# A decoder layer in float32 pairs: the first norm's weight row loaded once and spread by two TensorE products

## The chip, the cores and the metric

One core of a Trainium2 chip runs the kernel. The time is device microseconds of one execution; for each kernel the median of several runs is given.

## The reference

Input x has 512 tokens of 1024 channels. One layer is computed, all in float32:

```
h = rms_norm(x, norm_mix_pre)                     # x * rsqrt(mean(x*x) + 1e-6) * weights
z = h @ w_in                                      # 1024 x 10240, ten parts of 1024 columns
y_a, y_c, y_s = three causal branches of z        # short conv, long conv, spatial gating
m = (sum over branches of sigmoid(gate) * (y @ w_branch)) @ w_out
x = x + rms_norm(m, norm_mix_post)
h = rms_norm(x, norm_ffn_pre)
x = x + rms_norm(square(relu(h @ w_ff1)) @ w_ff2, norm_ffn_post)
```

The change touches only the first line. The first of the ten parts of `w_in` that the kernel multiplies is `s_v` (the `v` of the spatial gating).

## The kernel before

Every large product is made from two rounded parts of each operand, hi and lo, in three TensorE products (hi*hi, hi*lo, lo*hi; lines 1440 to 1444). Weights come in **units** of 128x1024 (512 KB) through two `raw` slots. ScalarE rounds a unit to `w_hi` (`split_hi`, line 607, its copy in line 605), VectorE subtracts and writes `w_lo` (`split_lo`, line 962, line 958), and a ring of four such pairs feeds TensorE. A unit's `raw` slot may be loaded again once its `w_lo` is written.

The start of the program, up to the first matmul of `s_v`, goes for each token tile c of 128 tokens through all engines:

- SyncE (line 420 on) loads x tile 0 into `resid` (its memory is called conf in the profile), then the weight row of the first norm, broadcast from one row of 4 KB in memory to 128 partitions, `row[0]` (its memory is glu; 512 KB are moved, line 429), then units 0 and 1, x tile 1, and with waits for `w_lo` the next units and tiles.
- ScalarE sums the squares of the tile (`sum_squares`, line 629), rounds a unit, and rounds the turned tile to `a_hi` (`turned_hi`, line 633). The order is written out in lines 642 to 654: for tile 0 squares, unit 0, `a_hi`, unit 1.
- POOL (GpSimd) makes rstd from the sum in two small steps (lines 512 and 516).
- VectorE multiplies x by rstd and by the weight row (lines 989 to 991, into `by_token`, whose memory is wide), makes `w_lo`, and `a_lo` of the turned tile (line 980).
- TensorE first runs 20 products of constants (`keep_warm`, line 1512), then turns tile 0 (8 transposes of 128x128, `turn`, line 1477), runs 6 more products of constants, and then blocks of `s_v`: a block (c, n) is token tile c by unit n, 6 matmuls. The order of the blocks and where the turns of tiles 1, 2, 3 stand between them is a table (`V_BLOCKS`, `V_TURNS`, line 49): (0, 0), (0, 1), turn of tile 1, (0, 2), and so on. The blocks of unit n wait for its `w_lo`, those of tile c for its `a_lo`.

Each engine goes through its own list in order. After `s_v` follow the other parts of `w_in`, the branches, `w_out`, and the MLP, which uses a Strassen-like scheme of seven products instead of eight on quarter blocks.

Of the kernel before, what the change touches and what calls it, by code (L numbers as in the profile page):

```python
# [25 lines left out]
F32 = mybir.dt.float32  # L26
F32R = mybir.dt.float32r
ALU = mybir.AluOpType
ACT = mybir.ActivationFunctionType

P = 128
D = 1024
# [3 lines left out]
HALF = D // 2  # L36
# [8 lines left out]
RAW = 2  # L45


WARM, WARM_AGAIN = 20, 6
V_BLOCKS = ((0, 0), (0, 1), (0, 2), (1, 0), (1, 1), (1, 2), (0, 3), (1, 3), (2, 0), (2, 1), (2, 2), (2, 3),
            (3, 0), (3, 1), (3, 2), (3, 3))  # L50
V_TURNS = {(0, 1): 1, (1, 2): 2, (2, 1): 3}
# [11 lines left out]
ROW_MIX_PRE, ROW_MIX_POST, ROW_FFN_PRE, ROW_FFN_POST = range(4)  # L63
# [151 lines left out]
def build(nc, x_d, units_d, cols_d, rows_d, ws_d, bs_d, out_d):  # L215
    kept_d = nc.dram_tensor("mixed_kept", (SEQ, D), F32, kind="Internal").ap()
    with ExitStack() as ctx:
# [10 lines left out]
        def sem(name):  # L228
            return ctx.enter_context(nc.semaphore(name))
# [9 lines left out]
        a_hi = sb("a_hi", [P, KT, SEQ], F32R)  # L239
# [6 lines left out]
        by_token = wide[:, :].rearrange("p (c n) -> p c n", c=CH)  # L246
# [5 lines left out]
        row = [glu_flat[:, n * D:(n + 1) * D] for n in range(3)]  # L252
# [5 lines left out]
        resid = conf_flat[:, :].rearrange("p (c n) -> p c n", c=CH)  # L258
# [16 lines left out]
        ones = sb("ones", [P, P], F32R)  # L275
# [6 lines left out]
        rstd = sb("rstd", [P, 4 * CH])  # L282
        power = sb("power", [P, CH])
        ps = ctx.enter_context(nc.psum_tensor("ps", [P, 8, 512], F32))
# [41 lines left out]
        x_loaded = [sem(f"x_loaded{n}") for n in range(CH)]  # L326
        x_again = sem("x_again")
        rows_loaded = sem("rows_loaded")
        rows_again = sem("rows_again")
        cols_loaded = sem("cols_loaded")  # L330
        spatial_loaded = [sem(f"spatial_loaded{n}") for n in range(2)]
# [8 lines left out]
        normed = sem("normed")  # L340
# [80 lines left out]
        def _(sp):  # L421
# [3 lines left out]
            def x_load(c):  # L425
                sp.dma_start(resid[:, c, :], x_d[c * P:(c + 1) * P, :]).then_inc(x_loaded[c], 16)

            x_load(0)
            sp.dma_start(row[0], rows_d[ROW_MIX_PRE:ROW_MIX_PRE + 1, :].to_broadcast([P, D])
                         ).then_inc(rows_loaded, 16)  # L430
            for slot in range(RAW):
                load(slot, slot)
            x_load(1)
# [169 lines left out]
        def _(act):  # L603
# [3 lines left out]
            def split_hi(u, into=None, free=True):  # L607

                act.wait_ge(raw_loaded[u.raw], u.loads())
                if free and u.first >= RING:  # L610
                    act.wait_ge(unit_done, u.times(1, 1 - RING))
                copy_hi(w_hi[:, u.ring, :] if into is None else into,
                        raw[:, u.raw, :]).then_inc(w_hi_ready, 1)
# [19 lines left out]
            def turned_hi(n, c, dst, banks):  # L633

                for g in range(2):
                    act.wait_ge(turned, 2 * n + g + 1)
                    copy_hi(dst[:, 4 * g:4 * g + 4, c * P:(c + 1) * P],
                            ps[:, banks + g, :].rearrange("p (k t) -> p k t", k=4)
                            ).then_inc(act_hi_ready, 1)


            for c in range(CH):
                act.wait_ge(x_loaded[c], 16)
                sum_squares(c, resid[:, c, :].rearrange("p (b n) -> p b n", b=2),
                            ps[:, 2 * c:2 * c + 2, :])
                if c == 0:
                    split_hi(Count(0))
                elif c < CH - 1:
                    split_hi(Count(c + 1))
                    turned_hi(c, c, a_hi, 2 * c)  # L650
                if c == 0:
                    turned_hi(0, 0, a_hi, 0)
                    split_hi(Count(1))
            turned_hi(CH - 1, CH - 1, a_hi, 2 * (CH - 1))


# [298 lines left out]
        def _(dve):  # L955
# [26 lines left out]
                       hi[:, 4 * g:4 * g + 4, c * P:(c + 1) * P]).then_inc(act_lo_ready, 1)  # L982


            dve.wait_ge(rows_loaded, 16)
            for c in range(CH):
                dve.wait_ge(x_loaded[c], 16)
                dve.wait_ge(rstd_ready, c + 1)
                nc.vector.scalar_tensor_tensor(out=by_token[:, c, :], in0=resid[:, c, :],
                                               scalar=rstd[:, c:c + 1], in1=row[0], op0=ALU.mult,  # L990
                                               op1=ALU.mult).then_inc(normed, 1)
                if c < CH - 1:
                    split_lo(Count(c + 1 if c else 0))
                turned_lo(c, c, a_hi, a_lo, 2 * c)
                if c == 0:
                    split_lo(Count(1))
# [165 lines left out]
            for j in range(KT):  # L1162
# [19 lines left out]
                for t in SILU_TILES.get(j, ()):  # L1182
                    dve.wait_ge(silu_th, t + 1)
                    nc.vector.scalar_tensor_tensor(out=nrm[:, t, :], in0=conf[:, t, :], scalar=1.0,
                                                   in1=nrm[:, t, :], op0=ALU.add,
                                                   op1=ALU.mult).then_inc(silu, 1)
# [44 lines left out]
            for c in range(CH):  # L1231
                if c == CH - 1:
                    x_turned(c - 1)
                for half in range(2):
# [7 lines left out]
                                               scalar=rstd[:, CH + 2 * c:CH + 2 * c + 1],  # L1242
                                               in1=resid[:, c, :], op0=ALU.mult,
# [193 lines left out]
        def _(pe):  # L1437
# [74 lines left out]
            def keep_warm(many):  # L1512
                for _ in range(many):
                    nc.tensor.matmul(ps[:, 7, :], ones[:, :], ones[:, :].unsqueeze(1).to_broadcast([P, CH, P]),
                                     start=True, stop=True)

            pe.wait_ge(consts_ready, 4)
            keep_warm(WARM)
            pe.wait_ge(consts_ready, 5)
            turn(0, 0, 0)  # L1520
            keep_warm(WARM_AGAIN)
            for c, n in V_BLOCKS:
                pe.wait_ge(act_lo_ready, 2 * c + n // 2 + 1)
                ready(Count(U_V + n))
# [199 lines left out]
```

## Time and profile before

| | before |
|---|---|
| median of 3 runs | 977.22 us (977.0 to 978.5) |
| the profiled execution, its time | 977.74 us |
| its span, first to last instruction | 976.0 us |
| TensorE (PE) busy | 959.6 us, 98% |
| VectorE (DVE) busy | 717.2 us, 73% |
| ScalarE (ACT) busy | 422.6 us, 43% |
| GpSimd (POOL) busy | 121.0 us, 12% |
| memory traffic | 135.43 MB read, 4.19 MB written |
| mean granted clock of TensorE | 0.996 |

The profile shows one execution. Busy time is counted per instruction; PEld is TensorE's loading of the stationary operand, and SPq, POOLq and the like are the engines' queues, which issue DMAs. A chain of waits is followed back from an instruction to what released it.

### The profile page before, as it was taken

The numbers are of one execution on the slowest core, as the hardware profiler recorded it, in microseconds if no ns is written. First come the engines' busy times: TensorE is split into PE (matmuls) and PEld (weight loads), VectorE is DVE, ScalarE is ACT, GpSimd is POOL, SyncE is SP. The second block draws the span as 40 slices with busy tenths as digits, with TensorE's granted clock in tenths as the row PEclk, the third lists the DMA queues.
The fourth block names the chain that finished last, engine by engine and source line by source line (L and its number), as shares of the span: only waits on it lengthen the run. The fifth ranks groups of instructions, "written<-read, shape, count | busy, mean of one in ns | idle before, by whom it ended". The sixth has DMA issues, their size and how long they took to land.

```text
span 976.0 us, 13542 instructions
## 1 busy us (share of the span) xinstructions
PE 959.6 (98%) x4910; PEld 819.0 (84%) x4910; DVE 717.2 (73%) x839; ACT 422.6 (43%) x526; POOL 121.0 (12%) x146
## 2 busy tenths in 40 slices
PE   8999999999999999999999999998899999999996
PEld 6888888888888888888888888898779989989985
DVE  5458889889888888886585434587775785796698
ACT  5333332333233222224374223466736745754673
POOL 1100000001000001122200000131122112111112
PEclk9999999999999999999999999999999999999999
DMA  6324222232232222224225333479989979989665
GB/s 244 96 87 130 92 91 92 89 110 91 95 104 86 87 86 86 86 87 139 99 86 216 108 107 108 172 169 283 235 197 222 229 197 233 195 195 259 140 177 141
DMA packets 39196, 140.23 MB, mean 144 GB/s; under 512 B 4464, under 2 KB 4592, under 8 KB 39152
## 3 DMA queue, kind: packets, MB, share of 16 engines
q1 hardware_dynamic: 28608, 101.88, 30.6%
q0 software_dynamic: 9728, 34.61, 19.3%
q10 hardware_dynamic: 816, 3.15, 0.9%
q8 instruction: 28, 0.46, 0.2%
q14 instruction: 16, 0.13, 0.0%
HBM read 135.43 MB, written 4.19 MB: 143 GB/s over the span
## 4 chain that ended last, share of the span: by engine, by line
PE 86%; DMA 5%; DVE 4%; ACT 3%; issue 1%; POOL 0%; DVEq 0%; POOLq 0%; SPq 0%; ACTq 0%
PE ps L1440 24%; PE ps L1442 24%; PE ps L1444 24%; PE ps L1607 4%; PE ps L1611 4%; PE ps L1609 4%; DMA raw_d<-units_in 4%; DVE w_lo L958 2%; ACT w_hi L605 1%; DVE h_lo L958 1%; DMA raw<-units_in 1%; PE ps L1483 1%; DVE wide L1306 0%; ACT h_hi L605 0%; PE ps L1548 0%
## 5 line engine op out<-in xcount | busy, mean ns | idle before, releaser
L1440 PE MATMUL ps<-a_hi,w_hi 128*128 128x512 f32 x576 | 225.4, 391 | 0.0
L1442 PE MATMUL ps<-a_lo,w_hi 128*128 128x512 f32 x576 | 224.2, 389 | 0.0
L1444 PE MATMUL ps<-a_hi,w_lo 128*128 128x512 f32 x576 | 224.1, 389 | 0.0
L958 DVE TENSOR_TENSOR w_lo<-raw,w_hi 128x1024 fp32r<-128x1024 f32 x124 | 153.1, 1237 | 89.5 <-ACT w_hi L605 89.1
L605 ACT ACTIVATE w_hi<-raw 128x1024 fp32r<-128x1024 f32 x124 | 130.2, 1056 | 188.5 <-PE ps L1444 111.0
L1034 DVE SCALAR_TENSOR_TENSOR conf<-glu,cols,conf (+1 forms) x240 | 186.9, 779 | 27.5 <-DVE conf L1034 26.4
L1442 PEld LDWEIGHTS ps<-a_lo,w_hi 128*128 128x128 f32 x576 | 108.2, 188 | 22.7 <-issue 0.5
L1440 PEld LDWEIGHTS ps<-a_hi,w_hi 128*128 128x128 f32 x576 | 108.1, 188 | 22.7 <-DVE w_lo L958 0.2
L1444 PEld LDWEIGHTS ps<-a_hi,w_lo 128*128 128x128 f32 x576 | 108.1, 188 | 22.5
L958 DVE TENSOR_TENSOR w_lo<-glu,w_hi 128x1024 fp32r<-128x1024 f32 x56 | 67.9, 1224 | 41.6 <-ACT w_hi L605 41.6
L1440 PE MATMUL ps<-w_hi,h_hi 128*128 128x512 f32 x224 | 87.8, 392 | 1.6 <-DVE wide L1306 0.8
L1442 PE MATMUL ps<-w_lo,h_hi 128*128 128x512 f32 x224 | 87.2, 390 | 0.0
L1444 PE MATMUL ps<-w_hi,h_lo 128*128 128x512 f32 x224 | 87.2, 389 | 0.0
L605 ACT ACTIVATE w_hi<-glu 128x1024 fp32r<-128x1024 f32 x56 | 58.6, 1054 | 46.8 <-PE ps L1444 20.4
L1607 PE MATMUL ps<-x_plain_hi,w_hi 128*128 128x256 f32 x256 | 73.7, 288 | 4.0 <-DVE h L1281 2.5
L1611 PE MATMUL ps<-x_plain_hi,w_lo 128*128 128x256 f32 x256 | 73.1, 286 | 0.0
L1609 PE MATMUL ps<-x_plain_lo,w_hi 128*128 128x256 f32 x256 | 73.1, 285 | 0.0
L576 POOL DMA_DIRECT2D glu<-units_in x40 | 34.8, 878 | 183.4 <-DVE w_lo L958 138.6
L1607 PE MATMUL ps<-x_diff_hi,w_hi 128*128 128x256 f32 x192 | 54.7, 285 | 1.2 <-DVE x_diff_lo L958 0.8
L1609 PE MATMUL ps<-x_diff_lo,w_hi 128*128 128x256 f32 x192 | 54.3, 283 | 0.0
L1611 PE MATMUL ps<-x_diff_hi,w_lo 128*128 128x256 f32 x192 | 54.3, 283 | 0.0
L1607 PEld LDWEIGHTS ps<-x_plain_hi,w_hi 128*128 128x128 f32 x256 | 49.8, 195 | 5.1 <-DVE h L1281 2.9
(175 smaller groups left out, 1655.7 us busy)
## 6 DMA issues: line engine op xcount, KB each, us to landing
raw<-units_in SPq DMA_DIRECT2D x128, 512.0 KB, 3.3
glu<-units_in POOLq DMA_DIRECT2D x40, 512.0 KB, 6.7
glu<-units_in SPq DMA_DIRECT2D x24, 512.0 KB, 5.3
raw_d<-units_in POOLq DMA_DIRECT2D x24, 512.0 KB, 8.3
raw_v<-units_in SPq DMA_DIRECT2D x16, 512.0 KB, 5.6
raw_d<-units_in SPq DMA_DIRECT2D x8, 512.0 KB, 3.9
conf<-x_in SPq DMA_DIRECT2D x4, 512.0 KB, 4.7
conf<-x_in ACTq DMA_DIRECT2D x1, 2048.0 KB, 7.9
```

Source lines behind the costliest of these rows:

```text
L576: pool.dma_start(slots[slot], units_d[source(u, added=True)], accum_op=ALU.add).then_inc(raw_added[slot], 16)
L605: return nc.scalar.activation(dst, src, ACT.Copy, scale=scale)
L958: return nc.vector.tensor_tensor(dst, src, hi, ALU.subtract)
L1034: nc.vector.scalar_tensor_tensor(out=conf[:, tile, :], in0=glu[:, tile, k:k + SEQ], scalar=cols[:, tile, COL_CONF + k:COL_CONF + k + 1], i ...
L1440: nc.tensor.matmul(ps[:, bank, :], left_hi, right_hi, start=first, stop=False, skip_group_check=on_top)
L1442: nc.tensor.matmul(ps[:, bank, :], left_hi, right_lo, start=False, stop=False, skip_group_check=on_top)
L1444: return nc.tensor.matmul(ps[:, bank, :], left_lo, right_hi, start=False, stop=final, skip_group_check=on_top)
L1483: mm = nc.tensor.transpose(ps[:, banks + g, k * P:(k + 1) * P], by_token[:, c, at:at + P], ident[:, :])
L1607: nc.tensor.matmul(out, w_hi[:, u % RING, w], hi[:, k, :], start=not free and k == 0, stop=False, skip_group_check=free)
L1609: nc.tensor.matmul(out, w_hi[:, u % RING, w], low[:, k, :], start=False, stop=False, skip_group_check=free)
L1611: mm = nc.tensor.matmul(out, w_lo[:, u % RING, w], hi[:, k, :], start=False, stop=k == CH - 1, skip_group_check=free)
```

## The change

It does four things. The weight row is loaded as one row of 4 KB to partition 0 of `row[1]`, ahead of all other loads. TensorE spreads it: after 4 products of constants it waits for that load and multiplies a column of ones (one partition) by the row in two products of 512 columns, into PSUM banks 4 and 5; then 8 products of constants, the turn of tile 0, 4 products of constants (instead of 20, the turn, and 6). VectorE's norm product of tile 0 reads the weights from these banks; for tiles 1 to 3 it reads `row[0]` as before, which ScalarE copies from the banks behind the squares of tile 1. And ScalarE rounds unit 1 ahead of `a_hi` of tile 0 instead of behind it.

```diff
-WARM, WARM_AGAIN = 20, 6
+WARM = 4, 8, 4
...
+        row_spread = sem("row_spread")
+        row_ready = sem("row_ready")
...
+            sp.dma_start(row[1][0:1, :], rows_d[ROW_MIX_PRE:ROW_MIX_PRE + 1, :]).then_inc(rows_loaded, 16)
             x_load(0)
-            sp.dma_start(row[0], rows_d[ROW_MIX_PRE:ROW_MIX_PRE + 1, :].to_broadcast([P, D])
-                         ).then_inc(rows_loaded, 16)
...
                 if c == 0:
                     split_hi(Count(0))
+                    split_hi(Count(1))
+                    turned_hi(0, 0, a_hi, 0)
                 elif c < CH - 1:
+                    if c == 1:
+                        nc.scalar.activation(row[0].rearrange("p (b n) -> p b n", b=2), ps[:, 4:6, :],
+                                             ACT.Copy).then_inc(row_ready, 1)
                     split_hi(Count(c + 1))
                     turned_hi(c, c, a_hi, 2 * c)
-                if c == 0:
-                    turned_hi(0, 0, a_hi, 0)
-                    split_hi(Count(1))
...
-            dve.wait_ge(rows_loaded, 16)
+            two = "p (b n) -> p b n"
             for c in range(CH):
                 dve.wait_ge(x_loaded[c], 16)
                 dve.wait_ge(rstd_ready, c + 1)
-                nc.vector.scalar_tensor_tensor(out=by_token[:, c, :], in0=resid[:, c, :],
-                                               scalar=rstd[:, c:c + 1], in1=row[0], op0=ALU.mult,
-                                               op1=ALU.mult).then_inc(normed, 1)
+                if c == 0:
+                    dve.wait_ge(row_spread, 1)
+                else:
+                    dve.wait_ge(row_ready, 1)
+                nc.vector.scalar_tensor_tensor(out=by_token[:, c, :].rearrange(two, b=2),
+                                               in0=resid[:, c, :].rearrange(two, b=2),
+                                               scalar=rstd[:, c:c + 1],
+                                               in1=row[0].rearrange(two, b=2) if c else ps[:, 4:6, :],
+                                               op0=ALU.mult, op1=ALU.mult).then_inc(normed, 1)
...
             pe.wait_ge(consts_ready, 4)
-            keep_warm(WARM)
+            keep_warm(WARM[0])
+            pe.wait_ge(rows_loaded, 16)
+            for b in range(2):
+                mm = nc.tensor.matmul(ps[:, 4 + b, :], ones[0:1, :].bitcast(F32), row[1][0:1, b * HALF:(b + 1) * HALF],
+                                      start=True, stop=True)
+            mm.then_inc(row_spread, 1)
+            keep_warm(WARM[1])
             pe.wait_ge(consts_ready, 5)
             turn(0, 0, 0)
-            keep_warm(WARM_AGAIN)
+            keep_warm(WARM[2])
```

ScalarE's list from its second row on, before (names are the memories of the program; `glu` holds the weight row):

```order
2 L630 ACTIVATE ps,sumsq<-conf 128x1024
3 L605 ACTIVATE w_hi<-raw 128x1024
4 L605 ACTIVATE a_hi<-ps 128x4x128 x2
5 L605 ACTIVATE w_hi<-raw 128x1024
6 L630 ACTIVATE ps,sumsq<-conf 128x1024
7 L605 ACTIVATE w_hi<-raw 128x1024
8 L605 ACTIVATE a_hi<-ps 128x4x128 x2
```

The same place now (the lines have moved by one or more):

```order
2 L631 ACTIVATE ps,sumsq<-conf 128x1024
3 L606 ACTIVATE w_hi<-raw 128x1024 x2
4 L606 ACTIVATE a_hi<-ps 128x4x128 x2
5 L631 ACTIVATE ps,sumsq<-conf 128x1024
6 L653 ACTIVATE glu<-ps 128x1024
7 L606 ACTIVATE w_hi<-raw 128x1024
8 L606 ACTIVATE a_hi<-ps 128x4x128 x2
```

The rounding of unit 1 now stands ahead of the two of `a_hi`, and the copy of the row stands between the squares of tile 1 and the rounding of unit 2.

TensorE's list at its start, before:

```order
1 L1514 MATMUL ps<-ones 128x512 x20
2 L1483 MATMUL ps<-ident,wide 128x128 x8
3 L1514 MATMUL ps<-ones 128x512 x6
4 L1440 MATMUL ps<-w_hi,a_hi 128x512
5 L1442 MATMUL ps<-w_lo,a_hi 128x512
```

And now:

```order
1 L1523 MATMUL ps<-ones 128x512 x4
2 L1530 MATMUL ps<-glu,ones 128x512 x2
3 L1523 MATMUL ps<-ones 128x512 x8
4 L1492 MATMUL ps<-ident,wide 128x128 x8
5 L1523 MATMUL ps<-ones 128x512 x4
6 L1449 MATMUL ps<-w_hi,a_hi 128x512
7 L1451 MATMUL ps<-w_lo,a_hi 128x512
```

The two products that spread the row, and eight products of constants, stand between the first four and the turn of tile 0. VectorE's list has the same instructions in the same order; only the sources and the waits of the norm products differ.

## Rows read from the trace of the kernel before

**Rows 1.** Busy time by engine in one stretch, then clock, DMA share, GB/s.

```profile
16.00:649.00 633.00, 633.00 (x2888) 526.28 (x2889) 464.53 (x584) 225.92 (x310) 58.83 (x63) 1.00 0.33 107
```

**Rows 2.** The chain of waits, 0 to 60 us: start, duration, what.

```profile
1.72 6.17 DMA raw<-units_in
7.91 1.06 ACT w_hi L605
...
9.94 0.95 ACT w_hi L605
...
13.39 1.30 DVE wide L989
14.73 1.09 PE ps L1483 x8
15.96 0.47 PE ps L1440
```

**Rows 3.** The timeline, 0 to 22 us: start, duration, engine, line, what.

```profile
0.81 0.38 SPq L426 DMA_DIRECT2D conf<-x_in  x1
...
1.25 0.42 SPq L429 DMA_DIRECT2D glu<-rows_in  x1
...
1.38 6.72 PE L1514 MATMUL ps<-ones 128*128 128x512 f32 x20 [1.38 <-POOL ones L498]
...
4.32 1.03 ACT L630 ACTIVATE ps<-conf 128x1024 f32<-128x1024 f32 x1 [2.23 <-DMA conf<-x_in]
...
6.58 1.28 DVE L989 SCALAR_TENSOR_TENSOR wide<-conf,rstd,glu 128x1024 f32<-128x1024 f32 x1 [6.58 <-POOL rstd L516]
...
8.87 1.07 ACT L605 ACTIVATE a_hi<-ps 128x512 fp32r<-128x512 f32 x2
8.99 1.22 DVE L958 TENSOR_TENSOR w_lo<-raw,w_hi 128x1024 fp32r<-128x1024 f32 x1 [1.13 <-ACT w_hi L605]
...
10.14 1.28 DVE L958 TENSOR_TENSOR a_lo<-ps,a_hi 128x512 fp32r<-128x512 f32 x2
...
10.88 0.50 PE L1440 MATMUL ps<-w_hi,a_hi 128*128 128x512 f32 x1 [0.41 <-DVE a_lo L958]
...
11.34 1.22 DVE L958 TENSOR_TENSOR w_lo<-raw,w_hi 128x1024 fp32r<-128x1024 f32 x1
...
13.48 1.06 ACT L605 ACTIVATE w_hi<-raw 128x1024 fp32r<-128x1024 f32 x1 [1.57 <-DMA raw<-units_in]
...
13.93 0.39 PE L1444 MATMUL ps<-w_hi,a_lo 128*128 128x512 f32 x1
...
15.42 1.09 ACT L605 ACTIVATE a_hi<-ps 128x512 fp32r<-128x512 f32 x2 [0.88 <-PE ps L1483]
...
16.05 1.29 DVE L958 TENSOR_TENSOR a_lo<-ps,a_hi 128x512 fp32r<-128x512 f32 x2 [0.24 <-ACT a_hi L605]
```

**Rows 4.** Landings: units 0 and 1; the row broadcast; the spatial weights.

```profile
DMA to landing us min/median/max: 6.2/6.6/7.0
...
DMA to landing us min/median/max: 5.2/5.2/5.2
...
DMA to landing us min/median/max: 2.0/2.1/2.6
```

**Rows 5.** The stretch between the landings of the broadcast and of unit 0.

```profile
6.50:7.90 1.40, 1.40 (x7) 0.95 (x6) 1.28 (x1) 0.00 (x0) 0.00 (x0) 1.00 1.03 421
```

**Rows 6.** The first products of constants, by tile; a float32 product, from the chain.

```profile
L1514 PE MATMUL ps<-ones x8: 628/628/792, 1.4 to 4.5; 128*128 128x512 f32 x8
...
441.50 0.86 PE ps L1568 x2
```

**Rows 7.** Groups on VectorE by form: one subtraction from SBUF, one from PSUM.

```profile
L958 DVE TENSOR_TENSOR v_lo<-wide,v_hi 128x512 fp32r<-128x512 f32 x8 | 5.5, 686 | 0.0
...
L958 DVE TENSOR_TENSOR a_lo<-ps,a_hi 128x512 fp32r<-128x512 f32 x8 | 5.1, 685 | 4.5 <-ACT a_hi L605 4.5
```

**Rows 8.** Busy time and clock in a later stretch.

```profile
687.00:691.00 4.00, 3.36 (x17) 3.37 (x18) 2.06 (x3) 2.56 (x3) 1.50 (x3) 0.63 0.46 137
```

## The prediction

> **What bounds the kernel.** I read the busy time by stretches first. From 16 to 649 us the matrix engine (PE) is busy the whole of 633 us [rows 1]. A microsecond won before 16 us is therefore kept that long, and behind that the waits are counted from work that starts earlier by as much. So only the first 16 us are in question, in which the change lies. There the chain of waits [rows 2] is to be read: it leads from the landing of the first weight unit (issued 1.72, landed 7.89) over ScalarE (w_hi of unit 0, a_hi of token tile 0, w_hi of unit 1 in 0.95 us, then the squares of tile 1) and the two small POOL steps to VectorE's norm product of tile 1 (13.39), the turn of tile 1 on PE (14.73) and block (0, 2) at 15.96, from which PE is never idle. Last I read the timeline of the same stretch [rows 3], for what stands beside that chain and how much room it has. I name the tiles 0 to 3 and units 0, 1, 2 by their numbers.
>
> **Part by part: the loads.** The 512 KB broadcast leaves SyncE's queue, and a 4 KB load goes in front. x tile 0 was issued at 0.81 and the next DMA at 1.25, so tile 0 is issued 0.44 us later and, its 3.5 us being unchanged, lands at 4.75 instead of 4.3 [rows 3]. Units 0 and 1 are issued as before but 508 KB less stand ahead of them. The broadcast landed at 1.25 + 5.2 = 6.45, 2.15 us behind tile 0; unit 0 came at 7.89, 1.45 later, and unit 1, issued about 0.44 behind it, at about 2.17 + 7.0 = 9.2, 1.3 later [rows 4]. With the broadcast gone I add the last two steps to 4.75: unit 0 at 6.2, unit 1 at 7.5. If the second transfer in the stream is slow wherever it comes from, its step is 2.15, and unit 1 lands at 8.2; if nothing is won, 9.2 or, with the extra issue, 9.6. I take 7.5, since the stream ran at 421 GB/s behind the broadcast [rows 5].
> The Trainium skill (DMA: Bandwidth & Descriptors, Specifications) puts the ceiling of the fabric at 435 GB/s; an estimate from it is 1.2 us for the removed 512 KB, and unit 1 would land at 9.2 + 0.44 - 1.2 = 8.4. By that rule the sum below would be -0.4 us instead of -0.75; the rows show a slower broadcast than that (2.15 us).
>
> **The spread.** Four warm-up products end at 1.38 + 4 x 0.44 = 3.1; at this point matmuls stand 0.44 us apart (8 of them from 1.4 to 4.5), which is the 1.2 GHz level, and the remaining 12 of the 20 take what is left of 6.72 us, so some 0.23 to 0.27 us [rows 3, 6]. The granted clock column shows 1.00 from the start; the level I take from the spacing. The 4 KB row lands 2.0 us (the shortest landing that I found) to 3.5 us (tile 0's own) after 0.81 [rows 3, 4], so between 2.8 and 4.3; I take 3.2. No row has a product over one partition: the nearest is a float32 product of 128x512, 0.86 us at full clock [rows 6], so two take 1.72, or 3.44 at half clock. With the clock up at 4.5 the spread ends at about 5.7, with it down all the time at 6.6. VectorE needs it at 7.02 (below): no cost, with 0.4 to 1.3 us to spare. Behind it 8 warm-ups (1.8 us) end at about 7.5, ahead of the turn at 8.36: none either.
>
> **The norm product of tile 0.** It waited for rstd at 6.58, 2.26 us after ScalarE began on tile 0; it starts 0.44 later, at 7.02. It reads PSUM now: the same subtraction of 128x512 takes 686 ns from SBUF and 685 ns from PSUM [rows 7], so I price that at nothing, with the range 0 to 0.07.
> The Trainium skill (VectorE: DVE Perf Modes, The TRN2 errata) gives a PSUM source 62 cycles more than an SBUF one, which at its clock is an estimate of 0.065 us; the sum by it would be -0.68 in place of -0.75. The pair of rows does not agree with it, and the measurement decides.
> Norm to turn is 1.34 us and turn to a_hi 0.69 (13.39, 14.73, 15.42) [rows 2, 3]: the turn of tile 0 starts at 8.36 and a_hi at 9.05, against 8.87 before: **+0.18, rounded 0.2 us**.
>
> **The split moved on ScalarE.** w_hi of unit 1 stood between a_hi and the squares of tile 1 and took 0.95 us of the chain [rows 2]. Now it lies ahead of a_hi. Squares of tile 0 run 4.75 to 5.9, w_hi of unit 0 6.2 to 7.2, of unit 1 7.5 to 8.5; a_hi is not ready before 9.05, so this costs nothing with 0.55 us of room. **-0.95 us.** The squares of tile 1 thus start 0.75 earlier, at about 10.0. Tile 1 itself has to be in: it landed before 10.8 and comes earlier too.
>
> **The copy of the row.** 1.06 us of ScalarE (a 128x1024 copy, the 7.91 row), behind the squares, from 11.2 to 12.3. The norm product of tile 1 waits for it, but also for rstd, at 13.39 - 0.75 = 12.64. Hidden, by 0.3 us. Behind the copy waits w_hi of unit 2, which was held by its load: 4.49 us after w_lo of unit 0 began (8.99, 13.48). That subtraction now starts right behind the norm product, at 8.25, so w_hi of unit 2 starts at 12.74 and ends at 13.8; VectorE comes to it at 13.84. Hidden, by a hair.
>
> **PE's two blocks before the turn of tile 1.** a_lo of tile 0 starts 0.63 behind a_hi (15.42, 16.05), at 9.68, 0.46 earlier than before; block (0, 0) starts 0.74 behind, at 10.42, and block (0, 1), which follows w_lo of unit 1, also moves by 0.46. Its last matmul began at 13.93 and now begins at 13.47, ahead of the turn of tile 1 at 13.98. VectorE ended w_lo of unit 1 at 12.56, now 12.1, before 12.64. So the 0.75 stays whole: block (0, 2) starts at 15.21 instead of 15.96.
>
> **Sum**: +0.2 - 0.95 = **-0.75 us**. The profiled execution took 977.74 us over a span of 976.0, so 976.99 of its kind; it stands 0.52 above the median of the runs, 977.22, and the forecast is set against that: **976.5 us**. That is 0.08%. A measurement of this kernel can tell about 0.2%, 1.95 us, so no change should be seen.
>
> **Rivals.**
> (a) *Unit 1 lands late and ScalarE stands on it.* The split of unit 1 now blocks a_hi. From a landing after 8.1 on, each microsecond costs one; at 8.83 the gain is gone, and at 9.2 a_hi starts at 10.2: +0.4 us, 977.6. For it: the stream is full from 2 us on, and tile 0 goes out later. Against it: half a megabyte fewer are in front. Chance 0.15; half of it at the 8.2 to 8.4 above, about 976.8.
> (b) *Slower: PE's own queue.* The two products and 8 warm-ups stand ahead of the turn of tile 0, on an engine that at first runs at 1.2 GHz, and PE may idle while the row loads. From 3.2 us there is work of 3.43 us at full and 6.86 at half clock. If the level rises at T, it ends at 3.2 + 3.43 + (T - 3.2)/2: ahead of 8.36 up to T = 6.7, and the whole gain is lost at T = 8.2. If it stays low until 10 us or more, the turn starts at 10.1 (1.7 late), and blocks (0, 0) and (0, 1), 12 matmuls, take 0.2 us more each: another 2.4, so 4.2 us over the forecast, 980.7. For it: before, PE had run without a stop from 1.38 when the spacing changed at 4.5, and now it has a wait at 3.1. Against it: the wait is 0.1 us if the row lands at 3.2. Chance 0.09.
> (c) *Tile 0 is not late.* If a small load holds the queue less than 0.44 us, a_hi keeps its 8.87 or is earlier; up to -1.2 us, 976.0. Chance 0.12.
> (d) *The change does nothing at the end.* Later waits swallow or add some of it: at 687 to 691 us PE was granted 0.63 of its clock, behind an idle stretch [rows 8]. This time lay beside a DMA-bound chain, so its absence wins little, but the same fall in another place costs up to the 1.5 us that 4 us at 0.63 lose. The runs before spread over 977.0 to 978.5. Chance 0.12, at 977.2 to 978.5; 0.04 more that the same luck gives a run under 975.3.
> The forecast has the remaining 0.48.
>
> **Numbers.** The range reaches from 975.5 ((c) with a quiet run) to 978.3 ((a), and (d) without its worst part); outside lie (b) and the edges of (d). Faster by over 0.2% (under 975.27) would need 2 us, more than the 0.95 removed and 0.44 together: 0.05. Slower by over 0.2% (above 979.17) is (b) with its clock low, 0.08. Within: 0.87.
>
> **What would show it.** Right: ScalarE starts on tile 0 at about 4.75, both weight splits end by 8.6, a_hi at 9.05, the copy ends before rstd of tile 1, block (0, 2) starts near 15.2, and from there all rows are 0.75 earlier. Wrong: a wait of a_hi or w_hi for the raw load behind 8.1 (a); warm-up products still running at 8.4, or matmuls 0.43 us apart after 5 us (b); VectorE's first product waiting for the spread instead of rstd.

## The result, and the profile after

The changed kernel takes 979.87 us (median of 14 runs, 978.36 to 984.13) against 977.21 us for the kernel before in the same runs (14, 976.31 to 980.5). The ratio is 1.0025 [1.0017, 1.0033]: **slower by 0.25%, 2.4 us** (the two medians lie 2.66 us apart), where 976.5 us was forecast and a range up to 978.3. The profiled execution took 981.02 us over a span of 978.4, before 977.74 over 976.0. It moves 134.91 MB in where 135.43 were read, and its work is otherwise the same.

From 16 us on nothing is new: PE is busy 632.48 of 633 us, against all 633 [rows 1]; the 0.5 us are waits around the turn of tile 1, which before lay ahead of 16 us.

```profile
16.00:649.00 633.00, 632.48 (x2884) 525.65 (x2883) 465.60 (x585) 224.50 (x308) 56.98 (x62) 1.00 0.32 108
```

The chain of waits of the changed kernel, its first stretch (start, duration, what):

```profile
1.38 2.07 PE ps L1523 x4
3.45 3.71 PE ps L1530 x4
7.16 3.71 PE ps L1523 x8
10.87 1.72 PE ps L1492 x8
12.61 0.60 ACT a_hi L606
13.21 1.05 ACT ps L631 x2
14.34 0.82 POOL meansq L513
15.23 0.57 POOL rstd L517
15.89 1.29 DVE wide L996
17.23 1.10 PE ps L1492 x8
18.45 0.47 PE ps L1449
```

Before, this chain began with a DMA and went through ScalarE [rows 2]. Now its first 12.6 us are PE's own queue: 4 products of constants, the spread (a float32 product is two entries, so x4 are the two products), 8 of constants, the turn of tile 0. From 1.38 us on none of it waits for anything. The turn starts at 10.67 where it started at 8.01, and block (0, 2) at 18.45 where it started at 15.96 [rows 2]: 2.49 us, and the two spans differ by 2.4 us, so the whole of the loss lies here.

The timeline of the same stretch, the rows that answer to [rows 3]:

```profile
0.81 0.34 SPq L430 DMA_DIRECT2D glu<-rows_in  x1
1.21 0.37 SPq L428 DMA_DIRECT2D conf<-x_in  x1
...
4.43 1.03 ACT L631 ACTIVATE ps<-conf 128x1024 f32<-128x1024 f32 x1 [2.34 <-DMA conf<-x_in]
...
5.98 0.57 POOL L517 TENSOR_TENSOR rstd<-meansq,power 128x1 f32<-128x1 f32 x1
...
7.30 1.28 DVE L996 SCALAR_TENSOR_TENSOR wide<-conf,rstd,ps 128x1024 f32<-128x1024 f32 x1 [7.30 <-PE ps L1530]
8.30 1.06 ACT L606 ACTIVATE w_hi<-raw 128x1024 fp32r<-128x1024 f32 x1 [1.52 <-DMA raw<-units_in]
...
10.67 1.91 PE L1492 MATMUL ps<-ident,wide 128*128 128x128 f32 x8
11.76 0.60 ACT L606 ACTIVATE a_hi<-ps 128x512 fp32r<-128x512 f32 x1 [2.40 <-PE ps L1492]
...
12.61 0.60 ACT L606 ACTIVATE a_hi<-ps 128x512 fp32r<-128x512 f32 x1 [0.26 <-PE ps L1492]
...
13.85 1.22 DVE L961 TENSOR_TENSOR w_lo<-raw,w_hi 128x1024 fp32r<-128x1024 f32 x1
14.15 1.02 ACT L653 ACTIVATE glu<-ps 128x1024 f32<-128x1024 f32 x1
...
15.89 1.28 DVE L996 SCALAR_TENSOR_TENSOR wide<-conf,rstd,glu 128x1024 f32<-128x1024 f32 x1 [0.82 <-POOL rstd L517]
```

VectorE's first norm product waits for the spread, not for rstd, which was there at 6.55. It ends at 8.58, and the turn could have begun then; it began 2.1 us later, behind the 3.7 us of constants that stand between the spread and it. ScalarE stood idle 2.40 us for the turn.

The products on PE by tile (entries, duration in ns min/median/max, first and last start, forms):

```profile
L1492 PE MATMUL ps<-ident,wide x8: 415/421/421, 10.7 to 12.2; 128*128 128x128 f32 x8
L1530 PE MATMUL ps<-glu,ones x4: 1056/1056/1217, 3.4 to 6.1; 1*128 1x512 f32 x4
```

An entry of the turn takes 421 ns; in the kernel before it takes 273. The products of constants ahead of the turn start 0.43 us apart (0.59 us behind the first of them), as in the first 3 us of both kernels, where they last 628 ns [rows 6]. TensorE's clock has two levels here, 1.2 GHz (half) and 2.4 GHz (full), told by this spacing. It is still at 1.2 GHz during the turn, and the first two products at the spacing of the full clock (0.23 us) stand behind it, at 12.72 and 12.95. The clock column of the windows reads 1.00 throughout. This is rival (b).

In the kernel before the level rose later than the prediction has it. The row of [rows 6] covers the time up to 4.6 us only and so ends at 4.5. Behind it, in the stretches 4.6 to 5.35 and 5.9 to 8:

```profile
L1514 PE MATMUL ps<-ones x3: 602/628/628, 4.1 to 5.0; 128*128 128x512 f32 x3
L1514 PE MATMUL ps<-ones x10: 387/393/397, 5.6 to 7.7; 128*128 128x512 f32 x10
```

The products that start up to 5.0 still last over 600 ns, those from 5.6 on under 400: the level rose at about 5.4, not at 4.5.

### The profile page after: what moved, and what is told of

It is laid out like the page before. It is cut to its first block, busy times and chain, and to the rows that moved or that the text cites. A ratio compares the mean times of both kernels' runs of the same rounds, so it can differ in the third digit from the quotient of the medians.

```text
span 978.4 us, 13531 instructions
## 1 busy us (share of the span) xinstructions
PE 960.5 (98%) x4904; PEld 818.3 (84%) x4904; DVE 717.3 (73%) x839; ACT 423.6 (43%) x527; POOL 121.0 (12%) x146
## 3 DMA queue, kind: packets, MB, share of 16 engines
HBM read 134.91 MB, written 4.19 MB: 142 GB/s over the span
## 4 chain that ended last, share of the span: by engine, by line
PE 89%; DVE 4%; DMA 3%; ACT 2%; issue 1%; POOL 0%; DVEq 0%; POOLq 0%; ACTq 0%
PE ps L1449 25%; PE ps L1453 24%; PE ps L1451 24%; PE ps L1622 4%; PE ps L1626 4%; PE ps L1624 4%; DMA raw_d<-units_in 3%; DVE w_lo L961 2%; PE ps L1492 1%; ACT w_hi L606 1%; DVE h_lo L961 1%; PE ps L1523 1%; ACT h_hi L606 0%; PE ps L1530 0%; PE ps L1563 0%
## 5 line engine op out<-in xcount | busy, mean ns | idle before, releaser
L606 ACT ACTIVATE w_hi<-raw 128x1024 fp32r<-128x1024 f32 x124 | 130.1, 1056 | 186.3 <-PE ps L1453 113.1
L1449 PEld LDWEIGHTS ps<-w_hi,h_hi 128*128 128x128 f32 x224 | 42.0, 188 | 14.2 <-issue 3.8
```

Of the source, the lines that this page charges most:

```text
L606: return nc.scalar.activation(dst, src, ACT.Copy, scale=scale)
L1449: nc.tensor.matmul(ps[:, bank, :], left_hi, right_hi, start=first, stop=False, skip_group_check=on_top)
```

## The experiments

The place at which each kernel stands is given by four starts or ends of its trace, all in us: the start of the turn of tile 0 on PE, the end of `w_lo` of unit 1 on VectorE, the start of the norm product of tile 1, the start of block (0, 2), behind which PE has no more waits to speak of. The last column is the ratio of the times to those of the kernel before, run on the same chip. The kernels e9, e10, e12 and e14 leave the first norm's weights out of the result (1/8 in their place).

| kernel | turn 0 | w_lo 1 ends | norm 1 | block (0, 2) | ratio to before |
|---|---|---|---|---|---|
| before | 8.01 | 12.56 | 13.39 | 15.96 | 1 |
| after | 10.67 | 15.07 | 15.89 | 18.45 | 1.0025 [1.0017, 1.0033] |
| e3_before_one_partition | 10.67 | 14.91 | 15.75 | 18.32 | 1.0026 [1.0016, 1.0037] |
| e8_before_32_partitions | 10.67 | 15.21 | 16.05 | 18.62 | 1.0028 [1.0018, 1.0037] |
| e4_before_full_width | 8.78 | 12.71 | 13.55 | 16.12 | 0.9991 [0.9981, 1.0001] |
| e15_one_partition_when_warm | 9.28 | 13.27 | 14.11 | 16.68 | 0.9993 [0.9979, 1.0006] |
| e1_warm_8_6_4 | 11.52 | 15.90 | 16.71 | 19.28 | 1.0002 [0.9989, 1.0015] |
| e2_warm_4_0_4 | 8.73 | 13.17 | 13.99 | 16.56 | 0.9997 [0.9988, 1.0006] |
| e11_warm_4_3_2 | 8.73 | 13.16 | 13.98 | 16.55 | 1.0003 [0.9995, 1.0012] |
| e7_only_split_moved | 8.11 | 13.13 | 13.97 | 16.54 | 1.0003 [0.9994, 1.0012] |
| e9_full_width_constants | 8.27 | 11.98 | 12.81 | 15.37 | 0.9994 [0.9985, 1.0003] |
| e10_constants_old_split | 8.19 | 12.14 | 12.97 | 15.53 | 1.0003 [0.9993, 1.0012] |
| e12_constants_4_2_4 | 8.44 | 12.16 | 12.98 | 15.55 | 0.9998 [0.9989, 1.0006] |
| e14_norm_ahead_of_w_lo | 8.19 | moved | 12.27 | moved | 1.0008 [0.9993, 1.0023] |
| e5_spread_full_width | 10.47 | 14.19 | 15.01 | 17.57 | 1.0013 [1.0003, 1.0022] |
| e6_full_width_old_split | 9.99 | 13.95 | 14.78 | 17.34 | 1.0012 [1.0001, 1.0023] |
| e13_real_row_full_width | 8.10 | 12.10 | 12.92 | 15.48 | 0.9994 [0.998, 1.0008] |

The ratios tell 2 us from nothing, but not 0.5 us. Below that only the starts in the traces speak, each of one execution. From the start of block (0, 2) to the end of the span the sixteen traces that have this start take 958.1 to 961.0 us, so one execution's time alone does not tell 0.5 us either.

In the texts put down before the runs, theory N says that products over one partition keep the clock at its lower level; its rivals have other letters.

### Is it the products over one partition, or the queue's length?

In the kernel before, with all its loads and orders, PE's list is made like the changed one, with products of constants over one partition that wait for nothing:

```diff
-WARM, WARM_AGAIN = 20, 6
+WARM = 4, 8, 4
...
+            for b in range(2):
+                nc.tensor.matmul(ps[:, 4 + b, :], ones[0:1, :].bitcast(F32),
+                                 ones[0:1, :].bitcast(F32).unsqueeze(1).to_broadcast([1, CH, P]),
+                                 start=True, stop=True)
```

> The kernel before (512 KB broadcast, its order of loads and splits), only TensorE's head changed: 4 products of constants, two float32 products over ONE partition of constants without any wait, 8 products, the turn, 4 products. Theory N: the level stays at 1.2 GHz until about 12 us, the turn starts near 10.3 instead of 8.0, and the time is 2 us or more over before (979.5 or more; more than the change, as the 0.95 us of the moved split is not won). Theory W (the wait for the row and the pause it leaves held the level down): no wait here, the level rises at 4.5, the turn starts at about 8.0, time as before (977.2).

The same over all 128 partitions (`ones[:, :]`, `[P, CH, P]`), and over 32:

> As the run with one partition, but the two float32 products go over all 128 partitions. Theory N: the level rises near 4.5 us as before, the turn starts near 8.0, time as before (977.2 within 0.5). If instead what holds the level down is the form of the float32 product (four passes) or the smaller number of products of constants, then this one is as slow as the one-partition run.

> As the run with one partition, with 32 partitions. If what counts is how much of the array takes part, a quarter may still be too little: turn at 10 to 10.9, about 979.5. If any more than one partition is enough: turn by 9, about 977.

The timelines of the three, one partition:

```profile
3.38 3.78 PE L1520 MATMUL ps<-ones 1*128 1x512 f32 x4
...
7.09 3.78 PE L1514 MATMUL ps<-ones 128*128 128x512 f32 x8
...
10.67 1.35 PE L1483 MATMUL ps<-ident,wide 128*128 128x128 f32 x8
```

all 128 partitions:

```profile
3.25 3.62 PE L1520 MATMUL ps<-ones 128*128 128x512 f32 x4
...
5.88 3.07 PE L1514 MATMUL ps<-ones 128*128 128x512 f32 x8
...
8.78 1.03 PE L1483 MATMUL ps<-ident,wide 128*128 128x128 f32 x8
```

32 partitions:

```profile
3.38 3.78 PE L1520 MATMUL ps<-ones 32*128 32x512 f32 x4
...
10.67 1.70 PE L1483 MATMUL ps<-ident,wide 128*128 128x128 f32 x8
```

The number of the products and their columns are equal; only the partitions of their operands differ. Over one partition the kernel before becomes as slow as the changed one (1.0026 and 1.0025, each known to about 0.1%), with neither a wait nor another load: the turn at 10.67 in both. Over 128 the ratio shows no loss. So the loss comes with the half clock, the narrow products are what keeps it, and 32 partitions are no better than one. In the profile all three show PE busy without a gap up to the turn. One trace each could be luck, as the moment of the rise varies; but in the eight traces in which full-width products alone stand ahead of the rise and it can be placed, it came between about 4.5 and 7.3 us, and in the six with narrow ones ahead of the turn (after, e1, e2, e3, e8, e11) not before 10.9. Widths between 32 and 128 were not tried.

Do narrow products also let a clock fall that is up? Fifteen full products go ahead, then the two over one partition, then the turn (6 constants behind it):

```diff
-WARM, WARM_AGAIN = 20, 6
+WARM, WARM_AGAIN = 15, 6
...
+            for b in range(2):
+                nc.tensor.matmul(ps[:, 4 + b, :], ones[0:1, :].bitcast(F32),
+                                 ones[0:1, :].bitcast(F32).unsqueeze(1).to_broadcast([1, CH, P]),
+                                 start=True, stop=True)
```

> The kernel before with 15 products of constants, then two one-partition products without a wait, then the turn and 6 products. The level is up when they begin, at about 7. Theory N for the rise alone: they run at full clock (0.9 us each) and the level stays; turn at 8.9, block (0, 2) at 16.5 to 16.9, 0.5 to 0.9 us over before. If such products also let the level fall, the turn or the first blocks run at half clock, 2 us or more over before.

```profile
L1483 PE MATMUL ps<-ident,wide x13: 272/273/328, 9.3 to 15.9; 128*128 128x128 f32 x13
L1520 PE MATMUL ps<-ones x4: 587/587/692, 7.4 to 8.8; 1*128 1x512 f32 x4
```

They run at the full clock (587 ns each, not 1056), and the turn behind them too (273 ns). 1.9 us of them do not lower the level here. The full products ahead of them still stood 0.43 us apart up to 6.24, though this list begins as that of the kernel before: a rise at about 6.5, not 5.4.

### Changing only the table of the changed kernel

```diff
-WARM = 4, 8, 4
+WARM = 8, 6, 4
```

> The changed kernel with 8 products of constants ahead of the spread and 6 behind it (instead of 4 and 8). Theory N (TensorE does not reach 2.4 GHz through products over one partition; only full ones ahead of them count): 8 full products end at 4.8 us, where the level rose before; the spread runs at full clock, 1.8 us, ends by 6.8, the turn of tile 0 starts at about 8.2, block (0, 2) at about 15.0, time about 1 us under before (976.2). Theory Q (the level does not matter, there is simply too much work ahead of the turn): 14 instead of 12 products of constants, so at least as slow as the change, 980 or more.

In the other two the line is `WARM = 4, 0, 4` and `WARM = 4, 3, 2`:

> The changed kernel with no products of constants between the spread and the turn of tile 0. Theory N: the spread still ends at about 7.1 us at half clock, the turn starts at about 8.6 instead of 10.7, but the level has not risen and the first blocks run at 0.43 us a matmul, so only part of the 2.4 us comes back: about 978 to 979. Theory Q: nothing is ahead of the turn, all the loss is gone: 976.5 or less.

> The change itself (real row, one partition) with 3 products of constants between spread and turn and 2 behind the turn. They fit in the 1.6 us that PE stood idle in the 4, 0, 4 run ahead of the turn (8.7), so the turn stays at 8.7 and the level rises no later. Theory N: block (0, 2) at 15.8 to 16.6, time within 0.5 us of before, at best a little under it; 2.4 us under the change.

With 8 full products ahead of the spread the twelve times fall into two groups: eight within 976.35 to 977.27 and four within 978.39 to 981.59. The profiled one (979.34) is of the second, and its timeline shows how:

```profile
1.38 3.78 PE L1523 MATMUL ps<-ones 128*128 128x512 f32 x8 [1.38 <-POOL ones L499]
5.09 3.78 PE L1530 MATMUL ps<-glu,ones 1*128 1x512 f32 x4
8.79 2.93 PE L1523 MATMUL ps<-ones 128*128 128x512 f32 x6
11.52 1.88 PE L1492 MATMUL ps<-ident,wide 128*128 128x128 f32 x8
```

At 5.09 the level had not risen yet, and the narrow products then held it down up to the turn. That the first group are executions in which it had risen by then is my reading; no trace of one was taken. The grouping alone doesn't show it, as the kernel before has nine of its 35 times on the same chip above 978, too. But an estimate from the spans speaks for it: the eight have spans of 974.6 to 975.5, and with at least 958.1 us behind block (0, 2), the least in any trace, that block started by 17.5, not at 19.28. The expectation came out for neither theory: 976.2 or 980 were expected, and the median is 977.07, against 976.86 before. Without the 8 products (e2) the turn starts at 8.73, still at half clock, and the loss is gone: 977.05 where 978 to 979 were expected. The first block, expected at half clock, starts at 12.11, when the level has just risen. So the eight products that were to raise the clock cost the time: at half clock they take 3.71 us and stand ahead of the turn. It takes both, the half clock and the products ahead of the turn. Three products instead (e11) give the same 8.73: they fit into the time in which PE waits for VectorE in e2. Both leave nothing of the reference out.

### What the other parts of the change are worth

The split alone, in the kernel before: `split_hi(Count(1))` ahead of `turned_hi(0, 0, a_hi, 0)`.

> The kernel before with nothing changed but ScalarE's order: unit 1 rounded ahead of a_hi of tile 0. The broadcast of 512 KB stays, so unit 1 lands at about 9.2 and a_hi waits for it. Rival (a) of the forecast says a_hi at 10.2, squares of tile 1 at 11.2 instead of 10.8: 0.4 us slower. If unit 1 lands by 8.3 as in the change, a gain of 0.5 instead.

Unit 1 lands at 9.12, `a_hi` starts at 10.11 instead of 8.87, and block (0, 2) 0.58 us later. With the 508 KB still in front the moved split stalls ScalarE, as rival (a) has it.

The changed kernel with a spread over 128 partitions of constants, so that the clock is right, with nothing else altered but that the weights are left out, and the same with the split back in its old place:

```diff
-                mm = nc.tensor.matmul(ps[:, 4 + b, :], ones[0:1, :].bitcast(F32), row[1][0:1, b * HALF:(b + 1) * HALF],
+                mm = nc.tensor.matmul(ps[:, 4 + b, :], mean_of[:, :], ones[:, :].bitcast(F32).unsqueeze(1).to_broadcast([P, CH, P]),
```

> The change, row still loaded first and waited for, 4, 8 and 4 products of constants; but the two spread products go over all 128 partitions and multiply constants (1/1024 by 1), so the first norm's weights are replaced by 1/8: the weights are left out of the result. Theory N: the level rises between 4.5 and 7, the spread ends between 5.7 and 7, the turn of tile 0 starts at 8.4 to 9, block (0, 2) at 15.2 to 15.9, time 0 to 0.8 us under before. If the wait for the row or the amount of work ahead of the turn is the cause, it is as slow as the change (+2.4).

> As the run with constants, but unit 1 rounded behind a_hi of tile 0 as before. The forecast's term: the moved split is worth 0.95 us of the chain, so block (0, 2) is 0.95 later than in the run with constants, about 16.1 to 16.8.

> As the run with constants, with 2 products of constants instead of 8 ahead of the turn. If the queue ahead of the turn still costs something in the run with constants, the turn is earlier here (8.2 to 8.4) and block (0, 2) at 15.1; if the turn waits for the norm product there already, no difference.

In e12 the spread took longer than in e9 (3.62 us for 2.84, the same list), so the norm product waited for it until 7.01 and the turn starts at 8.44; with only two constants between them, nothing more was lost.

With the clock right the changed kernel gains 0.59 us of block (0, 2) (15.37 for 15.96), where 0.75 was forecast; a gain too small for the ratio. But it doesn't come from the place I gave. With the split back (e10) 0.43 us of it remain. As the turn of tile 0 itself varies, the distance from it to block (0, 2) tells the split better: 7.10 and 7.11 us with the moved split (e9, e12), 7.34 with the old one (e10). The split is worth about 0.24, not 0.95. The rows of VectorE and POOL show why, in e9:

```profile
10.77 1.21 DVE L961 TENSOR_TENSOR w_lo<-raw,w_hi 128x1024 fp32r<-128x1024 f32 x1
...
11.15 0.92 POOL L513 TENSOR_SCALAR meansq<-sumsq 128x1 f32<-128x1 f32 x1 [4.40 <-ACT ps L631]
```

and in e10:

```profile
10.91 1.23 DVE L961 TENSOR_TENSOR w_lo<-raw,w_hi 128x1024 fp32r<-128x1024 f32 x1
...
12.01 0.23 POOL L513 TENSOR_SCALAR meansq<-sumsq 128x1 f32<-128x1 f32 x1 [5.34 <-ACT ps L631]
```

and in the kernel before:

```profile
11.34 1.22 DVE L958 TENSOR_TENSOR w_lo<-raw,w_hi 128x1024 fp32r<-128x1024 f32 x1
...
12.01 0.62 POOL L512 TENSOR_SCALAR meansq<-sumsq 128x1 f32<-128x1 f32 x1 [5.57 <-ACT ps L630]
```

POOL's step takes 0.23 us for tile 0. For tile 1 it is stretched in ten of the traces, to 0.62 up to 0.93 us, and then it ends 0.07 to 0.10 us behind the end of VectorE's subtraction, whenever it began: at 12.07 behind 11.98 in e9 (0.92 us long), 12.63 behind 12.56 before (0.62). In e10 it takes its 0.23 us; there the squares set it, and it ends 0.10 behind the subtraction too (12.24 behind 12.14), because both follow `w_hi` of unit 1 on ScalarE. So do e3, e4, e6, e8 and e15, all with the old split. ScalarE's squares were ready 0.86 us earlier in e9 than in e10, and the step ended 0.17 earlier: the subtraction took the place of the squares. In all the traces but e14's the norm product of tile 1 starts 0.81 to 0.84 us behind the end of `w_lo` of unit 1 (table). The test is to take the subtraction out of the way: e9 with `split_lo(Count(1))` moved behind the norm product of tile 1.

> The run with constants (weights left out, 1/8 in their place), with VectorE's w_lo of unit 1 moved behind the norm product of tile 1. Theory L (POOL's first small step cannot end while VectorE subtracts w_lo: in every trace so far it ends 0.07 to 0.10 us behind that subtraction, whether it began 0.8 us or 0.1 us earlier): now the step takes 0.23 us, and the norm product of tile 1 starts 1.1 us behind the end of the squares, at about 12.1 instead of 12.8. Rival S (the squares and POOL alone set it, as I read the chain): the step stays at 0.8 to 0.9. Block (0, 1) comes late, so the time itself gets 1 to 2 us worse; only the steps count.

```profile
11.31 0.23 POOL L513 TENSOR_SCALAR meansq<-sumsq 128x1 f32<-128x1 f32 x1 [4.64 <-ACT ps L631]
...
14.84 0.47 PE L1449 MATMUL ps<-w_hi,a_hi 128*128 128x512 f32 x1 [2.71 <-DVE w_lo L961]
...
16.44 1.91 PE L1492 MATMUL ps<-ident,wide 128*128 128x128 f32 x8
```

The step takes 0.23 us again, and the norm product starts at 12.27, 0.54 earlier than in e9, although the squares ended 0.16 later. So VectorE's subtraction held POOL. (VectorE did nothing else beside this step; whether another instruction would hold it was not tried.) As a version it is no use: PE stands idle 2.71 us ahead of block (0, 1), and the next turn then runs at half clock (1.91 us for 1.09).

### A complete version with the clock right

The row must be spread over 128 partitions of operands: VectorE zeroes `row[1]`, the row lands in partition 0, and 128 rows of ones by it give the same sum. First with the row on ScalarE's queue, with the new and the old place of the split:

```diff
-WARM = 4, 8, 4
+WARM = 9, 6, 4
...
-            sp.dma_start(row[1][0:1, :], rows_d[ROW_MIX_PRE:ROW_MIX_PRE + 1, :]).then_inc(rows_loaded, 16)
...
+            act.wait_ge(row_zeroed, 1)
+            act.dma_start(row[1][0:1, :], rows_d[ROW_MIX_PRE:ROW_MIX_PRE + 1, :]).then_inc(rows_loaded, 16)
...
+            nc.vector.memset(row[1], 0.0).then_inc(row_zeroed, 1)
...
-                mm = nc.tensor.matmul(ps[:, 4 + b, :], ones[0:1, :].bitcast(F32), row[1][0:1, b * HALF:(b + 1) * HALF],
+                mm = nc.tensor.matmul(ps[:, 4 + b, :], ones[:, :].bitcast(F32), row[1][:, b * HALF:(b + 1) * HALF],
```

> The change with the spread made over all 128 partitions: VectorE first zeroes the buffer (about 1.1 us while it is idle), ScalarE's queue loads the 4 KB row into partition 0 of it, and the two products take the whole buffer, behind 9 products of constants (6 behind). Everything else is as in the change. Theory N (only products over one partition kept the clock down): the level rises between 4.5 and 6, the spread ends by 7, the turn of tile 0 starts at 8 to 8.5, block (0, 2) at 15.0 to 15.3, and the 0.75 to 1.1 us of the forecast come: about 976.0 against 976.9 of the kernel before. If the forecast was wrong in more than the clock, block (0, 2) stays at 15.9 or later though the turn is on time.

> As the full-width spread, but ScalarE's order of before: unit 1 is rounded behind a_hi of tile 0. By the forecast's sum the moved split is the whole gain (0.95 us of the chain): block (0, 2) 0.95 later than in the full-width run, time as before or up to 0.2 over it. Rival: the row copy or rstd sets the norm product of tile 1 anyway, then it differs by less than 0.5.

```profile
2.04 0.53 ACTq L644 DMA_DIRECT2D glu<-rows_in  x1
...
6.92 1.98 PE L1533 MATMUL ps<-glu,ones 128*128 128x512 f32 x4 [1.33 <-DMA glu<-rows_in]
```

The rows are of e5. A miss: 4 KB issued at 2.04, behind tile 0 and both units, took 4.8 us to land, and the norm product starts at 9.04 (e6: 4.4 us, 8.57). Both are slower than the kernel before, by 0.13% and 0.12%. The old split was to be 0.95 later at block (0, 2) and is 0.23 earlier, as its row landed earlier; from the turn of tile 0 on the pair repeats the one above, 7.10 us with the moved split and 7.35 with the old. Then with the row on SyncE's queue between tile 0 and the units (`sp` for `act`, `WARM = 7, 4, 4`):

> A complete version with the spread over 128 partitions: VectorE zeroes the buffer (1.1 to 2.0 us), SyncE issues x tile 0, then behind that wait the 4 KB row, then units 0 and 1; 7, 4 and 4 products of constants. The row lands behind tile 0 at about 4.4, the products run 4.6 to 6.4 (8.0 if the level is still low), the turn starts at 8.1 to 9, block (0, 2) at 15.3 to 15.9: within 0.6 us under the kernel before, and 2.5 to 3 us under the change. If the row lands at 5.5 or later, as from ScalarE's queue, the turn is at 9.5 and it is 0.5 to 1 us over before.

```profile
2.03 0.31 SPq L433 DMA_DIRECT2D glu<-rows_in  x1
...
4.53 2.00 PE L1533 MATMUL ps<-glu,ones 128*128 128x512 f32 x4
...
8.10 1.06 PE L1495 MATMUL ps<-ident,wide 128*128 128x128 f32 x8 [0.65 <-DVE wide L999]
```

Here block (0, 2) starts at 15.48, 0.48 us ahead of the kernel before, and the ratio, 0.9994 [0.998, 1.0008], cannot be told from 1. Of the complete versions of the change it has the earliest block (0, 2); its ratio lies 0.31% under that of the change as made, but can't be told from those of e2 and e11 (0.9997, 1.0003), which change nothing but the table.

## Why the prediction was wrong

- **The spread, and the 8 products behind it**, are the step that failed: "with the clock up at 4.5 the spread ends at about 5.7, with it down all the time at 6.6 ... no cost. Behind it 8 warm-ups (1.8 us) end at about 7.5, ahead of the turn at 8.36". The spread ended at about 7.2, and the 8 products took 3.7 us and held the turn until 10.67. Two things were wrong. With the clock down the sum priced only the spread at half clock, not the 8 products; at 6.6 + 3.7 = 10.3 they would have stood in the way there too. And I took the time at which the level had risen before for a property of the clock, when it was one of the work in front of it: 20 products over 128 partitions. With products over 1 partition among them it had not risen at 10.67 (e3). The time itself was misread: 4.5 is the end of the row, the rise came at about 5.4.
- **Rival (b)** named the right mechanism, with its place and the turn at 10.1 (measured 10.67), and had 0.09. I weighed it by PE's wait for the row ("the wait is 0.1 us"); there was no wait, and e3 shows that it needs none. It names no partitions; that the narrow products are the cause is what e3 and e4 add. Its price was too high, 980.7 for 979.87: it let the blocks (0, 0) and (0, 1) run at half clock, 2.4 us, and the level rose behind the turn, so they ran at 0.23 us. In exchange the spread at half clock takes 3.71 us and not 3.44, as a one-partition product is not quite the float32 product of [rows 6] (some 1.9 us for the two at the full clock, from 7.4 to 9.28 in e15, for 1.72). Two of its sums are off by 0.1 us, without weight for the outcome: 1.7 and 2.4 are 4.1, not 4.2, and a spread from 3.2 on with the clock up at 4.5 ends at 5.6, not 5.7.
  The Trainium skill (TensorE: Matmul & The Clock Gate, Part 1) says that the clock follows how busy the engine has been recently. Busy as the profile counts it does not decide: PE is busy without a gap up to the turn in e3 and e4, and only e4's clock rises ahead of it.
- **The bound** holds: a start later by 2.49 us at block (0, 2) is 2.4 us at the end. That the two agree so well is partly luck, as the rest of the program varies by up to 2.9 us from one execution to another.
- **The loads.** Tile 0, forecast 0.44 late, was 0.11 late in this pair of traces (ScalarE begins at 4.43 for 4.32), but that is luck of the pair: ScalarE begins at 4.39 to 4.63, on average 4.54, in the eight traces with the 4 KB load in front, and at 4.04 to 4.34, on average 4.20, in the six with the loads of before. The forecast is nearly right, and rival (c) did not come true. The start of `w_hi` of unit 0 (5.73) fits the 6.2 or better; unit 1 came at 8.3, not 7.5, and at 7.5 to 8.6 in the other traces with these loads.
  By the 435 GB/s of the Trainium skill (DMA: Bandwidth & Descriptors, Specifications) the estimate had been 8.4, near the 8.3 of this trace. The traces don't bear out its 1.2 us for unit 0, which came over 2 us earlier (5.7 for 7.9).
- **The split, -0.95 us**, is mis-assigned; it measured about 0.24. The chain of waits led over ScalarE's squares and POOL, and I read each link as a cause. POOL's step could not end before VectorE's `w_lo` of unit 1, which was bound by the landing of unit 0 and the `a_lo` ahead of it. The row that could have warned was in the trace: 0.62 us for a step that takes 0.23 for tile 0.
  The Trainium skill (GPSIMD Engine Reference, Specifications) says that POOL shares its SBUF interfaces with VectorE and contends with instructions that have two SBUF inputs. The trace agrees as far as it goes: `w_lo` has two, and without it beside the step, in e14, the step takes 0.23 us. An instruction with one such input was not tried.
- **The norm product from PSUM** was priced at nothing: 1279 ns from PSUM for tile 0, 1283 from SBUF for tile 1, in the changed kernel. The 62 cycles of the Trainium skill (VectorE: DVE Perf Modes, The TRN2 errata) are not seen.
- **The copy of the row** and `w_hi` of unit 2 stayed hidden, as forecast; in e9 they end before anyone asks.

That the sum (-0.75) and the gain with the clock right (-0.59) are near each other is mostly chance: one term was too large (the split), and one was given no price (the earlier unit 0 lets `w_lo` of unit 1 end 0.58 earlier, which the prediction puts at 0.46 but counts as hidden).

## What to carry to other kernels

Warm-up products are only worth what they raise: check from the spacing of the products that the level is up where the first real work starts, and keep products over few partitions behind that point, or widen them with zeroes. While TensorE may still be at half clock, every warm-up product ahead of real work costs double (0.43 us for 0.23); let the real work go first. And in a chain of waits, look at the duration of each small step beside the same step elsewhere: one that is stretched may be held by a neighbour, and shortening what is in front of it then gives nothing.

## What the hardware showed that I had not expected

- Products over 1 and over 32 partitions, back to back on a busy PE, do not raise TensorE's clock, nor do the eight full ones behind them up to the turn (turn at 10.67, +0.26% and +0.28%), while the same number over 128 do (8.78). Once the level is up they run at it, and it stays up over the 1.9 us tried (e15).
- The moment of the rise varies from one execution to the next. In e9, e10, e12 and e14 PE's list is the same up to the end of the spread, and its four entries, begun at 3.25, took 2.84, 2.50, 3.62 and 3.19 us. The kernel before, e7 and e15 begin with the same products of constants, and the level rose at about 5.4, 5.8 and 6.5.
- The granted clock reads 1.00 in stretches in which the products last 628 ns and stand 0.43 us apart.
- A 128x1 step on POOL takes 0.23 us alone and up to 0.93 beside a subtraction on VectorE, and ends 0.07 to 0.10 us behind it.
- 4 KB took 4.8 and 4.4 us to land (e5, e6) when issued on ScalarE's queue behind 1.5 MB, though it is 1/128 of a unit; issued at the same time on SyncE's queue ahead of the two units it was in within 2.5 us (e13). Which of the two it is, the queue or the place, was not separated.
